# Up projection of a hybrid layer: four of 22 pairs of tiles by seven block products in place of eight

## What is computed

```python
h = rmsnorm(x, g_ffn)
up = h @ w_up
a, u = up[..., :D_FF], up[..., D_FF:]
a = causal_depthwise_conv(a, conv_w, conv_b)
x = x + (jax.nn.gelu(a) * u) @ w_down
```

## Time and profile before

| | |
|---|---|
| median of three runs | 883.51 us |
| the profiled execution | 883.9 us |
| its span, first to last instruction | 881.8 us |
| TensorE (PE) busy | 876.3 us, 99% |
| VectorE (DVE) busy | 607.3 us, 69% |
| ScalarE (ACT) busy | 437.1 us, 50% |
| GpSimd (POOL) busy | 9.2 us, 1% |

### The profile page before, as it was taken

One profiled execution on the slowest core, in us unless ns is written; L12 is line 12 of the kernel. 1 busy time (PEld: TensorE's weight loads), 2 busy tenths in 40 slices (PEclk: granted clock), 3 DMA queues, 4 the chain that ended last, 5 costly groups with the idle time before them and its releaser, 6 DMA issues.

```text
span 881.8 us, 12304 instructions
## 1 busy us (share of the span) xinstructions
PE 876.3 (99%) x4528; PEld 749.9 (85%) x4528; DVE 607.3 (69%) x815; ACT 437.1 (50%) x593; POOL 9.2 (1%) x15
## 2 busy tenths in 40 slices
PE   8999999999999999999999999999999999999998
PEld 6788898898898889999888888888888888998887
DVE  7897796796796886766556666677776556554745
ACT  7865766766764744434445333334433333422631
POOL 1200000000000000000000000000000000000000
PEclk9999999999999999999999999999999999999999
DMA  8233233233232232326322222222222325322241
GB/s 282 85 109 119 72 105 111 71 106 108 71 108 83 63 114 98 97 84 228 118 96 96 96 95 95 95 95 95 96 95 95 87 68 156 108 70 92 90 149 67
DMA packets 29829, 91.93 MB, mean 104 GB/s; under 512 B 4160, under 2 KB 5456, under 8 KB 29664
## 3 DMA queue, kind: packets, MB, share of 16 engines
q1 hardware_dynamic: 28496, 87.70, 30.5%
q10 hardware_dynamic: 1072, 3.67, 1.3%
q0 software_dynamic: 224, 0.06, 0.1%
HBM read 84.34 MB, written 2.10 MB: 98 GB/s over the span
## 4 chain that ended last, share of the span: by engine, by line
PE 98%; DMA 1%; DVE 0%; SPq 0%; issue 0%; ACT 0%; DVEq 0%
PE dense L555 26%; PE dense L556 26%; PE dense L557 26%; PE aty L556 3%; PE aty L557 3%; PE aty L555 3%; PE z L628 2%; PE z L557 2%; PE z L556 2%; PE z L555 2%; PE aty L661 1%; DMA fs<-in_xT 1%; PE aty L678 1%; PE aty L676 1%; DVE fs L1588 0%; PE z L616 0%
## 5 line engine op out<-in xcount | busy, mean ns | idle before, releaser
L555 PE MATMUL dense<-hi,w_hi 128*128 128x512 f32 (+1 forms) x940 | 366.6, 390 | 0.7 <-DVE lo L1591 0.6
L556 PE MATMUL dense<-lo,w_hi 128*128 128x512 f32 (+1 forms) x940 | 363.6, 387 | 0.0
L557 PE MATMUL dense<-hi,w_lo 128*128 128x512 f32 (+1 forms) x940 | 363.5, 387 | 0.0
L1588 DVE TENSOR_TENSOR w_lo<-w_f,w_hi 128x1024 fp32r<-128x1024 f32 (+3 forms) x152 | 171.4, 1131 | 92.4 <-ACT w_hi L1011 87.7
L555 PEld LDWEIGHTS dense<-hi,w_hi 128*128 128x128 f32 x940 | 176.7, 188 | 37.2 <-issue 1.6
L557 PEld LDWEIGHTS dense<-hi,w_lo 128*128 128x128 f32 x940 | 176.6, 188 | 36.1
L556 PEld LDWEIGHTS dense<-lo,w_hi 128*128 128x128 f32 x940 | 176.8, 188 | 33.7 <-issue 0.2
L1011 ACT CAST w_hi<-w_f 128x1024 fp32r<-128x1024 f32 (+3 forms) x128 | 125.5, 981 | 61.2 <-PE dense L557 48.8
L1588 DVE TENSOR_TENSOR fs<-fs 128x512 f32<-128x512 f32 (+3 forms) x137 | 101.1, 745 | 3.9 <-ACT fs L996 0.2
L996 ACT ACTIVATE fs<-fs 128x512 f32<-128x512 f32 (+2 forms) x85 | 59.8, 707 | 52.2 <-DVE fs L1591 37.3
L1588 DVE TENSOR_TENSOR lo<-fs,hi 128x512 fp32r<-128x512 f32 (+3 forms) x67 | 52.3, 792 | 23.9 <-ACT hi L1476 18.8
(11 more groups left out here) (156 smaller groups left out, 993.9 us busy)
## 6 DMA issues: line engine op xcount, KB each, us to landing
w_f<-in_w_in SPq DMA_DIRECT2D x52, 512.0 KB, 3.4
w_f<-in_w_up SPq DMA_DIRECT2D x44, 512.0 KB, 3.3
w_f<-in_w_down SPq DMA_DIRECT2D x16, 512.0 KB, 3.8
w_f<-in_w_b SPq DMA_DIRECT2D x8, 512.0 KB, 3.2
w_f<-in_w_out SPq DMA_DIRECT2D x8, 512.0 KB, 3.4
w_f<-in_w_pg SPq DMA_DIRECT2D x8, 512.0 KB, 3.3
w_f<-in_w_down SPq DMA_DIRECT2D x8, 384.0 KB, 3.6
fs<-in_xT SPq DMA_DIRECT2D x4, 512.0 KB, 7.5
```

The lines of the kernel that those rows point to most:

```text
L555: mm(out, w1, x1, start=start, stop=False, skip_group_check=skip)
L556: mm(out, w1, x0, start=False, stop=False, skip_group_check=skip)
L557: return mm(out, w0, x1, start=False, stop=stop, skip_group_check=skip)
L1588: return nc.vector.tensor_tensor(out, a, b, op).then_inc(done, 1)
```

## The change

Pairs 6, 9, 12 and 15 of the up stage become blocks: rows are the gate and the value tile, columns the first and the second 256 tokens of h. TensorE runs up_block in place of the 48 matmuls of the pair. The loops of the up stage are written out. The four combinations of h (16 sums, 8 casts, 8 low parts, each of 128x512) are formed by VectorE and ScalarE in steps 1 to 5. VectorE combines the products with two copies that ScalarE makes of the first two. The sums of g move from steps 10 to 15 to steps 16 to 21. DOWN_I takes the place of GATE_PAIRS in the down stage as the number of blocks that went before. SP's program is the same.

```diff
+UP_BLOCKS = (6, 9, 12, 15)
+DOWN_I = GATE_PAIRS + len(UP_BLOCKS)
...
+A_SU = (9, 13, 14, 15)
+A_USNAP = 17
+T_UFORM = {1: 30, 2: 28, 3: 26, 4: 24}
...
-            with pe.Fori(0, 7) as it:
-                for q in range(6):
-                    up(6 * it + (q + 2), (UP0 + 2 + q) % 3)
+            def up_block(n):
+
+                i, c = GATE_PAIRS + n, UP0 + 2 * UP_BLOCKS[n]
+                r1, r2, r3 = c % RING, (c + 1) % RING, (c + 2) % RING
+                pe.wait_ge(s_form, 5 * i + 1)
+                product(region(1), r1, 0, moving_h(0, 0), True)
+                pe.wait_ge(s_form, 5 * i + 2)
+                pe.wait_ge(s_utlo, 8)
+                product(region(2), r2, 0, moving_uform(1), True)
+                pe.wait_ge(s_usnap, 2 * n + 1)
+                product(region(1), r1, 4, moving_h(1, 0), False)
+                pe.wait_ge(s_form, 5 * i + 3)
+                product(region(3), r3, 0, moving_uform(2), True)
+                pe.wait_ge(s_form, 5 * i + 4)
+                pe.wait_ge(s_usnap, 2 * n + 2)
+                product(region(2), r1, 0, moving_h(1, 1), False)
+                pe.wait_ge(s_wlo, c + 2)
+                product(region(4), r2, 4, moving_uform(4), True)
+                pe.wait_ge(s_form, 5 * i + 5)
+                pe.wait_ge(s_ucomb, 6 * n + 1)
+                product(region(3), r2, 0, moving_uform(3), False)
...
+            def up_step(f):
+
+                c = UP0 + 2 * f
+                if f in UP_BLOCKS:
+                    n = UP_BLOCKS.index(f)
+                    i, r1, r2, r3 = GATE_PAIRS + n, c % RING, (c + 1) % RING, (c + 2) % RING
+                    act.wait_ge(s_used, c)
+                    high_weight_form(i, 2, 3, r3, 0)
+                    act.wait_ge(s_prod, 7 * i + 1)
+                    nc.scalar.copy(up_copy(0), region(1)).then_inc(s_usnap, 1)
+                    high_weight_form(i, 4, 4, r1, 0)
+                    act.wait_ge(s_prod, 7 * i + 2)
+                    nc.scalar.copy(up_copy(1), region(2)).then_inc(s_usnap, 1)
+                    high_weight_form(i, 3, 2, r2, 0)
+                    high_g(f - 1)
+                    high_behind(c + 2, 7 * i + 4, 8)
+                    high_behind(c + 3, 7 * i + 5, 8)
+                elif f + 1 in UP_BLOCKS:
+                    up_ahead(c + 2)
+                    high_g(f - 1)
+                    first_forms(GATE_PAIRS + UP_BLOCKS.index(f + 1), c + 2)
+                elif f - 1 in UP_BLOCKS:
+                    high_behind(c + 2, 7 * (GATE_PAIRS + UP_BLOCKS.index(f - 1)) + 7, 8)
+                    high_g(f - 1)
+                    up_ahead(c + 3)
+                else:
+                    up_ahead(c + 2)
+                    high_g(f - 1)
+                    up_ahead(c + 3)
                 conv_gelu(f)
...
+            for part in range(2):
+                a, b, e = A_GF[part]
+                up_step(2 * part + 1)
+                if part == 0:
+                    act.wait_ge(s_rst, 1)
+                high_uform(1, part, a, 3)
+                high_uform(3, part, b, 5)
+                up_step(2 * part + 2)
+                high_uform(2, part, a, 6)
+                high_uform(4, part, e, 8)
+            for f in range(5, 16):
+                up_step(f)
...
+            def second_sum(n):
+
+                i = GATE_PAIRS + n
+                dve.wait_ge(s_prod, 7 * i + 4)
+                dve.wait_ge(s_usnap, 2 * n + 1)
+                tt(a_pad[:, 2 + HALF:], region(3), up_copy(0), ALU.add, s_ucomb)
...
+            def up_step(f, between=None):
+
+                c = UP0 + 2 * f
+                if f in UP_BLOCKS:
+                    n = UP_BLOCKS.index(f)
+                    i, r1, r2, r3 = GATE_PAIRS + n, c % RING, (c + 1) % RING, (c + 2) % RING
+                    low_weight_form(i, 2, 2, r3, 0)
+                    low_weight_form(i, 4, 3, r1, 0)
+                    value(f - 1)
+                    low_weight_form(i, 3, 4, r2, 0)
+                    second_sum(n)
+                    up_ahead(c + 2)
+                    gate_block(n)
+                    up_ahead(c + 3)
+                    convolve(f)
+                    return
+                if f + 1 in UP_BLOCKS:
+                    low_first_weights(c + 2)
+                else:
+                    up_ahead(c + 2)
+                value(f - 1)
                 if between:
                     between()
+                if f + 1 in UP_BLOCKS:
+                    i = GATE_PAIRS + UP_BLOCKS.index(f + 1)
+                    weight_sums(i, c + 2)
+                    low_weight_form(i, 1, 1, (c + 3) % RING, 0)
+                    low_last_quarter(c + 3)
+                else:
+                    up_ahead(c + 3)
+                gate_path(f, c % 3)
...
+                def three_sums():
+                    if part:
+                        low_uform(2, 0, A_GF[0][0], 3)
+                        low_uform(4, 0, A_GF[0][2], 4)
+                    whole_h(a, 0, 0, part)
+                    whole_h(b, 0, 1, part)
+                    h_difference(a, b, a, base + 2)
+
+                def two_lows():
+                    low_uform(1, part, a, lows + 1)
+                    low_uform(3, part, b, lows + 2)
+                    dve.wait_ge(s_utlo, lows + 1)
+                    h_difference(a, e, a, base + 5)
+
+                up_step(2 * part + 1, three_sums)
+                whole_h(e, 1, 1, part)
+                h_difference(b, e, b, base + 4)
+                up_step(2 * part + 2, two_lows)
+                dve.wait_ge(s_usum, base + 6)
+                whole_h(e, 1, 0, part)
+                h_difference(e, e, a, base + 7)
...
+            up_step(5, last_lows)
+            for f in range(6, 16):
+                up_step(f)
```

More of the change, by code:

```diff
@@ L345, in g_part, with up_copy @@
             return t[:, k0:k0 + 2, col * HALF:(col + 1) * HALF]
+        def up_copy(half):
+            return fs[:, A_USNAP, half * HALF:(half + 1) * HALF]
         def two_halves(row):
@@ L1484, in _, with up_ahead @@
             conv_gelu(0)
[L1486 to L1496 removed]
+            def up_ahead(c):
+                high(c // RING, c % RING)
+            def up_step(f):
[26 more added lines that the diff above has]
+                    up_ahead(c + 3)
+                conv_gelu(f)
@@ new lines, in high_uform @@
+            def high_uform(n, part, row, done):
+                act.wait_ge(s_usum, 8 * part + done)
+                nc.scalar.copy(hi[:, T_UFORM[n] + part, :], fs[:, row, :]).then_inc(s_uthi, 1)
+            for part in range(2):
[8 more added lines that the diff above has]
+                high_uform(4, part, e, 8)
@@ L1504, in _ @@
                 nc.scalar.copy(g_part(hi, 0, 1, part), two_halves(b)).then_inc(s_gthi, 1)
-                up_step(3 + part, 2)
-            with act.Fori(5, 7) as it:
-                for q in range(3):
-                    up_step(it, q)
+                up_step(18 + 3 * part)
             def down_ahead(c):
@@ new lines, in gate_block @@
+            def gate_block(n):
+                i = GATE_PAIRS + n
+                dve.wait_ge(s_prod, 7 * i + 3)
+                tt(a_pad[:, 2:2 + HALF], region(1), rs[:, 0:HALF], ALU.mult, s_ucomb)
+                dve.wait_ge(s_prod, 7 * i + 5)
+                dve.wait_ge(s_ucomb, 6 * n + 1)
+                tt(a_pad[:, 2 + HALF:], region(2), a_pad[:, 2 + HALF:], ALU.add, s_ucomb)
+                dve.wait_ge(s_ucomb, 6 * n + 3)
+                tt(a_pad[:, 2 + HALF:], a_pad[:, 2 + HALF:], rs[:, HALF:SEQ], ALU.mult, s_read)
@@ new lines, in value_block @@
+            def value_block(n):
+                i, f = GATE_PAIRS + n, UP_BLOCKS[n]
+                u = fs[:, A_U, :]
+                dve.wait_ge(s_prod, 7 * i + 7)
+                tt(u[:, 0:HALF], region(3), up_copy(0), ALU.add, s_ucomb)
+                dve.wait_ge(s_usnap, 2 * n + 2)
+                dve.wait_ge(s_ucomb, 6 * n + 4)
+                tt(u[:, HALF:SEQ], u[:, 0:HALF], up_copy(1), ALU.add, s_ucomb)
+                dve.wait_ge(s_ucomb, 6 * n + 5)
+                tt(u[:, 0:HALF], region(4), u[:, 0:HALF], ALU.add, s_ucomb)
+                dve.wait_ge(s_ucomb, 6 * n + 6)
+                tt(u, u, rs, ALU.mult, s_read)
+                gated(f, u)
@@ new lines, in up_ahead, with value @@
+            def up_ahead(c):
+                low(c // RING, c % RING)
+            def value(f):
+                if f in UP_BLOCKS:
+                    value_block(UP_BLOCKS.index(f))
+                else:
+                    value_path(f, (UP0 + 1 + 2 * f) % 3)
+            def up_step(f, between=None):
+                c = UP0 + 2 * f
+                if f in UP_BLOCKS:
+                    n = UP_BLOCKS.index(f)
[8 more added lines that the diff above has]
+                    up_ahead(c + 3)
+                    convolve(f)
+                    return
+                if f + 1 in UP_BLOCKS:
+                    low_first_weights(c + 2)
+                else:
+                    up_ahead(c + 2)
```

(29 more changed lines are left out.)

63 lines of the change are left out of this document (31 added, 32 removed).

## The result

The changed kernel takes 906.75 us (median of six runs, 905.16 to 909.16), against 883.53 us (six runs, 883.43 to 883.64): 1.0267 times as long, 95% interval 1.0251 to 1.0283. The profiled execution took 907.16 us, of them 905.3 us of span.

The account below looks back on a forecast made before the run. TensorE's instruction stream was taken as the bound; waits of 1.0 + 1.5 + 5.8 + 3.7 + 10.0 = 22.0 us less 3.2 saved gave + 18.8: 902.7 us profiled, 902.3 median. Range 894 to 909, the forecast's own 899 to 906.

Parts of the forecast that it names:

- the third rival: TensorE's clock falls at the waits: 904.7 us with one 2.4 us loss, 914.3 behind all five long waits; chance 0.24.
- The saving: TensorE's seven-product blocks replace pairs of tiles: 10.08 against 10.88 us, saving 0.80 us each, 3.20 us over four.
- (a): Third product of the later three blocks waits for ScalarE's copy behind the convolution: 3.34 us each, 10.0 in all.
- (b): VectorE falls behind in steps 1 to 4 of the up stage; TensorE waits 1.0 us in step 4.
- x: Start of a step's first low part on VectorE, counted from its gate tile's start: 2.32 us growing to 11.1.
- (c): First block's start: its first product waits 1.5 us for a low part, its second 5.8 us for the first weight form.
- (d): First block's third product waits 3.7 us for ScalarE's copy, starting at 24.7 us where it was due at 21.04.
- After the last block and the down stage: VectorE's remaining lag is absorbed before the down weights are due: no wait taken, up to 2 us in the range.
- The clock: Possible fall of TensorE's clock after waits: nothing in the forecast's sum, treated only as a rival with 2.4 us a loss.
- The first rival: The change does what it says: TensorE loses 3.2 us and waits nowhere, 880.3 us; chance 0.04.
- The second: Rival: only the third-product waits hold, as VectorE keeps up in steps 1 to 5; + 10.2 us, 893.7 us; chance 0.12.

Follow-up runs that it names:

- the third experiment: Changed kernel with ScalarE's and VectorE's block-step queues both reordered: copy ahead of the convolution, low parts of the weight forms earlier; 892.46 us, 1.0091 of the kernel before.
- the last version: Changed kernel with both queues reordered, the last quarter's cast a tile earlier, and sums of h, g and weights in idle places; 880.63 us, 0.9961 of the kernel before.
- the second: Changed kernel with ScalarE's queue alone reordered, second weight form's cast and first product's copy ahead of the convolution and gelu; 899.07 us, 1.0169 of the kernel before.
- the first: Changed kernel with ScalarE's cast of the last quarter of a block's weights waiting for one tile earlier; 905.5 us, 1.0244 of the kernel before.
- the run with waits alone: Kernel before, no blocks in the up stage, VectorE repeating low parts in pairs 3 and 17 so TensorE stops among 512-wide matmuls; 902.35 us, one run.
- the sums experiment: Changed kernel with sums of h, g and weights moved into VectorE's idle places, block step's order kept; 900.11 us, 1.0178 of the kernel before.

## Why the prediction was right, and which term was off

The forecast for the profiled execution was 902.7 us, and it took 907.16; the median, 906.75, is 4.5 us over the forecast of 902.3. It lies inside the range of 894 to 909, but outside the forecast's own 899 to 906: the case that came was the third rival's (0.24), and what held it was the room that the range had left for losses of the clock. The waits themselves came out as worked out.

- **The saving**: 0.80 us a block, 3.2 in all. Right, shown by the third experiment's block of 10.08 us and by the last version, which gains 3.45 us and waits nowhere in the up stage.
- **(a)** 3.34 us a block: 3.31 measured in each of the three, with each link within 0.02 us. That it hangs on the copy's place is shown by the second and the third experiment; the first shortened it through the chain's first link. That the rest of the block hides behind this wait was right too, and once the wait was gone the fourth and seventh products showed what had been hidden.
- **(b)** x of 2.3, 4.5, 6.6, 10.0, 11.1: measured 2.4, 4.6, 6.6, 10.0, 11.05, and 1.0 us of wait in step 4. Right.
- **(c)** 1.5 and 5.8 us: 1.45 (with 0.4 of it already inside step 4) and 5.7. Right. The cause of (b) and (c) is the order, since the same operations moved into idle places leave nothing of either.
- **(d)** 3.7 us: 2.4. The product started when forecast (24.6 us against 24.7), but the second one before it ran at the low clock and took 1.2 us of the wait.
- **After the last block and the down stage**: nothing, as taken.
- **The clock** is the term that was off. The sum had it at nothing; it cost 5.9 us of slow matmuls, 1.2 of them inside the wait of (d), so 4.7 net, with 0.1 us a restart. The third rival had this, with 2.4 us a loss from the earlier trace rows; in the profiled execution the level was low behind the stops of the first, second and fourth block and not behind the third's. (The first matmuls of the kernel before start 0.427 us apart from 2.12 to 5.96 us, which is what the low level gave in the run with waits alone, while the granted clock from 1.5 to 6.5 us reads 1.00; so in that place the clock row does not show it.) The prediction's reason against this rival, that part of a loss hides, was right for 1.2 us and too small to carry. 902.7 + 4.7 + 0.4 = 907.8 against 907.16. The page of before had no stop of such length inside the work, and I put 0.24 on the rival that needed one. With five stops near or over 3 us ahead, at least one fall should have been the likeliest case: every profiled execution here with a stop of over 2.9 us has one.

The first rival, no wait at all, was not wrong about the amount of work, only about this order of it: its 880.3 us are the last version's 880.63. The second named its right condition (VectorE keeps up in steps 1 to 5), and once that was met by moving work, its sum held but for the clock: 884.08 - 3.2 + 4 x 3.31 = 894.1 us, and 6.8 us for the three falls make 900.9, against 900.76 in the profiled execution.

The spread of the changed kernel's runs, 4 us where that of the kernel before is 0.2, goes with the clock as well: the run of 905.16 us had a mean granted clock of 0.992, those of 908.72 and 909.16 had 0.987. Which stops were followed by a fall in those is not shown, since they have no trace.

## What to carry to other kernels

Where two in-order engines hand a tile back and forth, add up the time of the one hand-over that the bottleneck waits for, link by link from the rows, and see what stands ahead of it in each queue; busy shares (VectorE 72% in the changed kernel, 73% in the last version) say nothing about it. Work with a far due time belongs where an engine waits for the other one anyway, and not between two steps of the chain. A stop of TensorE near 3 us or longer should be priced with a half-clock stretch behind it, one and a half to three microseconds here, even if the profile of before has the clock at its full level everywhere.

## What the runs showed of the hardware that I had not expected

- **The fall is not certain, and has no sharp bound in these runs.** Distances of 3.43 us were followed by the low level in five of seven cases (blocks 2 and 4 of the changed kernel, not 3; blocks 1, 2 and 4 of the sums experiment, not 3), 3.40 was not, 2.92 was, 2.74 and everything under 1.5 us was not. The longer ones, 3.76, four of 5.8 and one of 11.2 us, all were. The Trainium skill ("TensorE: Matmul & The Clock Gate", section "Why this matters for your kernels") speaks of gaps of over about 3 us. The traces agree with the size, but not with a rule that could be counted on either way.
- **It can come late.** Behind the second block's wait the first ten matmuls ran at the full level (584.00 to 585.20), and only then did they start 0.213 us apart; behind others the low level was there at once. A late one lasted 16 matmuls of 256 columns each time, 1.5 us. One that was there at once lasted 13 (1.4 us, copy first), 26 or 27 (2.6 to 2.7 us), and with a second stop amid them 27 and 31 (2.5 and 2.9 us). Why is not shown.
- **A wait can hide a slow stretch, and a slow stretch part of a wait** (block 1, 1.2 us), so taking one away doesn't give its whole time back.
- **A stop has a small price of its own**: the first matmul behind one is followed after 0.23 us and not 0.12 (584.02 to 584.25) at the full clock, and after 0.38 and not 0.213 (541.83 to 542.21) at the low one.
